# First mixer of a three-block kernel in a new order: gated-delta inverse in two halves, weight blocks by halves between scan, attention and gated levels

## What is computed

```
def token_mix(h, w_in, ...):
    p = (h @ w_in).astype(jnp.float32)
    ...
    o_a = rms_norm(fox_attention(q, k, split_heads(v, FOX_HEADS), log_f), fox_on_g)
    ...
    # gated_delta_chunked: per chunk of 64 tokens, t_mat unit lower triangular
    w = lax.linalg.triangular_solve(t_mat, kb * jnp.exp(G)[..., None], ...)
    u = lax.linalg.triangular_solve(t_mat, v * beta[..., None], ...)
    def step(state, inp):
        v_new = ui - jnp.einsum('bhcd,bhde->bhce', wi, state)
        o = einsum(qi, state) + einsum(ai_qk, v_new)
        state = state * ai[..., None, None] + einsum(ki, v_new)
    ...
    # gla_chunked (hg and gla): decayed products of q and k under a causal mask, times v
x = x + mixed @ w_out[l]
```

## Time and profile before

| | us |
|---|---|
| median of 3 runs | 1157.44 (1156.89 to 1160.16) |
| the profiled execution, its time | 1161.16 |
| its span in the trace | 1159.4 |
| PE busy, share | 95% |
| DVE busy | 70% |
| ACT busy | 52% |
| mean granted TensorE clock, of full speed | 0.956 |

### The profile page before, as it was taken

The page is one execution under the profiler, slowest core; times in us unless marked ns, Lnnn a source line. Parts: engine busy times, 40 slices in busy tenths (PEclk is TensorE's granted clock), DMA queues, the critical chain, the costliest instruction groups (busy, mean ns, idle before and its releaser), DMA issues.

```text
span 1159.4 us, 22157 instructions
## 1 busy us (share of the span) xinstructions
PE 1099.8 (95%) x9104; PEld 1069.7 (92%) x9104; DVE 809.5 (70%) x1140; ACT 598.0 (52%) x782; POOL 5.3 (0%) x15
## 2 busy tenths in 40 slices
PE   6699997799999999999999999999999899999996
PEld 5699986699999999999899999998998899999995
DVE  4557633846877777776697877778875687877775
ACT  4753341325655545544564554567666565544564
POOL 0000000000000000000000000000000000000000
PEclk9699995769999999999999999999999999999998
DMA  8333320014545455455464555543633354555531
GB/s 314 110 110 109 110 73 1 3 48 149 186 178 192 170 189 184 164 194 205 125 214 165 191 195 181 181 138 121 214 137 119 109 184 145 207 192 170 192 109 37
DMA packets 25714, 174.29 MB, mean 150 GB/s; under 512 B 3069, under 2 KB 3349, under 8 KB 5296
## 3 DMA queue, kind: packets, MB, share of 16 engines
q1 hardware_dynamic: 25088, 171.63, 42.8%
q0 software_dynamic: 560, 1.70, 0.5%
HBM read 172.26 MB, written 1.06 MB: 149 GB/s over the span
## 4 chain that ended last, share of the span: by engine, by line
PE 68%; DVE 7%; ACT 3%; issue 2%; DVEq 0%; ACTq 0%
PE PS L416 37%; PE PS L453 30%; DVE w_lo L1649 3%; ACT w_hi L1099 2%; DVE arena L2159 1%; ACT arena L1403 1%; DVE arena L2163 1%; PE PS L851 1%; DVE arena L2177 0%; DVE x L2106 0%; PE PS L856 0%; PE PS L1013 0%; DVE arena L2100 0%; DVE arena L2191 0%; DVE h_lo L1662 0%
## 5 line engine op out<-in xcount | busy, mean ns | idle before, releaser
L1649 DVE TENSOR_TENSOR w_lo<-raw,w_hi 128x2048 fp32r<-128x2048 f32 x158 | 361.3, 2288 | 103.0 <-ACT w_hi L1099 101.5
L416 PE MATMUL PS<-h_hi,w_hi 128*128 128x256 f32 x1248 | 357.3, 286 | 9.4 <-DVEq L1643 6.8
L416 PE MATMUL PS<-h_hi,w_lo 128*128 128x256 f32 x1248 | 354.8, 284 | 0.0
L416 PE MATMUL PS<-h_lo,w_hi 128*128 128x256 f32 x1248 | 354.8, 284 | 0.0
L1099 ACT ACTIVATE w_hi<-raw 128x2048 fp32r<-128x2048 f32 x158 | 300.8, 1906 | 93.4 <-PE PS L453 47.7
L416 PEld LDWEIGHTS PS<-h_hi,w_hi 128*128 128x128 f32 x1248 | 241.0, 193 | 11.2 <-DVEq L1643 7.0
L416 PEld LDWEIGHTS PS<-h_lo,w_hi 128*128 128x128 f32 x1248 | 241.0, 193 | 0.3 <-issue 0.2
L416 PEld LDWEIGHTS PS<-h_hi,w_lo 128*128 128x128 f32 x1248 | 241.1, 193 | 0.0
L453 PE MATMUL PS<-act_hi,w_hi 128*128 128x256 f32 x720 | 203.4, 284 | 2.2 <-DVE act_lo L1679 2.2
L453 PE MATMUL PS<-act_hi,w_lo 128*128 128x256 f32 x720 | 203.6, 284 | 0.0
L453 PE MATMUL PS<-act_lo,w_hi 128*128 128x256 f32 x720 | 200.9, 284 | 0.0
(11 more groups left out here) (311 smaller groups left out, 1356.0 us busy)
## 6 DMA issues: line engine op xcount, KB each, us to landing
raw<-weights SPq DMA_DIRECT2D x158, 1024.0 KB, 4.9
arena<-masks_in SPq DMA_DIRECT2D x1, 1856.0 KB, 12.7
raw<-weights SPq DMA_DIRECT2D x2, 512.0 KB, 5.8
x<-x_in SPq DMA_DIRECT2D x4, 256.0 KB, 7.2
arena<-bias_by_distance POOLq DMA_DIRECT2D x1, 1024.0 KB, 6.0
result<-x SPq DMA_DIRECT2D x4, 256.0 KB, 2.1
arena<-p_in POOLq DMA_DIRECT2D x2, 256.0 KB, 4.2
row<-row_in SPq DMA_DIRECT2D x1, 390.0 KB, 8.1
```

The lines of the kernel that those rows point to most:

```text
L416: return pe.matmul(o, lhs, rhs, start=start, stop=stop)
L1649: tt(w_lo[:, slot, :], raw[:, slot, :], w_hi[:, slot, :].bitcast(F), ALU.subtract).then_inc(lo_ready, 1)
```

## The change

It touches the first mixer alone.

- **Loads.** SP issues `w_gk` and weight block 3 ahead of `row` and the masks, and blocks 4 and 5 behind them.
- **Block order.** hg_q is block 4, fox_q, fox_k and fox_v are 5 to 7, hg_f is 8; the tables of pieces are gone, and each engine's program is a written list. PE calls `project(n, f)` for half f of block n.
- **Inverse.** Masks, copies and subtractions go by halves of four units; `gdn_cx` and `gdn_xcx` take a half g. All five levels stand between the two halves of block 8.
- **Scan, attention, levels.** Blocks 9 to 14 are multiplied here: halves of 9 to 11 and the first of 12 between the pieces of scan and attention, the second half of 12 and blocks 13 and 14 between the levels.
- **Smaller pieces.** The new state takes two DVE instructions of 128 rows in place of four of 64, and isn't made after the last chunk; the gains of fox's q and k are applied by ACT in the copy of the turned rows; norms of the heads are taken for two groups at once; ScalarE's functions are grouped so that it loads its function table 4 times behind the start in place of 7; the pairs of gla lie in banks 2 and 3 together and not in 2 to 5, which leaves 4 and 5 to the weight blocks; the first two groups are turned ahead of the last values.

```diff
-MIX_ORDER = ("small", "gdn_q", "gdn_k", "gdn_v", "hg_f", "fox_q", "fox_k", "hg_q", "fox_v", "gla_qk",
-             "gla_v", "hg_i", "gdn_z", "hg_g", "gla_g")
+MIX_ORDER = ("small", "gdn_q", "gdn_k", "gdn_v", "hg_q", "fox_q", "fox_k", "fox_v", "hg_f", "gla_qk",
+             "hg_i", "gla_v", "gdn_z", "hg_g", "gla_g")
...
+            sp.dma_start(w_gk, w_gk_in).then_inc(sem("ident_and_channel"), 16)
+            weights_in(3)
             sp.dma_start(row[:, :], row_in.partition_broadcast(P)).then_inc(sem("mix_inputs"), 16)
-            sp.dma_start(w_gk, w_gk_in).then_inc(sem("mix_inputs"), 16)
             sp.dma_start(masks, masks_in).then_inc(sem("mix_inputs"), 16)
-
+            weights_in(4)
+            weights_in(5)
...
+            def gdn_cx(lv, g):
+
+                pe.wait_ge(sem("inv_ready"), 2 * lv + g + 1)
+                pe.wait_ge(sem("ct_ready"), 2 * lv + g + 1)
+                for u in range(4 * g, 4 * g + 4):
                     last = mm(bank2(2)[:, u, :], c_t[:, u, :], inv[:, u, :])
                 last.then_inc(sem("cx"), 1)
 
-            def gdn_xcx(lv):
-                pe.wait_ge(sem("cx_copied"), lv + 1)
-                pe.wait_ge(sem("inv_t_ready"), lv + 1)
-                if lv == 0:
-                    pe.wait_ge(sem("la_keys"), 1)
-                for u in range(8):
+            def gdn_xcx(lv, g):
+                pe.wait_ge(sem("cx_copied"), 2 * lv + g + 1)
+                pe.wait_ge(sem("inv_t_ready"), 2 * lv + g + 1)
+                for u in range(4 * g, 4 * g + 4):
...
             first_columns()
             mean_of_x(0, 6, sum_1, True)
-            for n, what in enumerate(MIX_ORDER):
-                if n < 2:
-                    continue
-                for piece in before.get(n, ()):
-                    piece()
-                if n > 2:
-                    pe.wait_ge(sem(f"proj_bank_read{n % 2}"), n // 2)
-                columns(n, n % RING, 4 + n % 2, (h_hi, h_lo), what in CHANNEL_MAJOR, middle=middle.get(n, ()))
+            project(2, 0)
+            turn_small()
+            gk_product()
+            project(2, 1)
+            project(3, 0)
+            gates()
+            project(3, 1)
...
+            project(6, 1)
+            gdn_channels()
+            project(7, 0)
+            gdn_grams()
+            project(7, 1)
+            gdn_turn_decay()
+            gdn_turn_m()
+            project(8, 0)
+            for lv in range(5):
+                gdn_cx(lv, 0)
+                gdn_cx(lv, 1)
+                gdn_xcx(lv, 0)
+                gdn_xcx(lv, 1)
+            project(8, 1)
+            gdn_solve()
+            fox_turn()
+            project(9, 0)
             gdn_state_in(0)
             fox_logits(0)
             gdn_state_out(0)
+            project(9, 1)
             gdn_state_in(1)
             fox_turn_probs(0)
             gdn_state_out(1)
+            project(10, 0)
...
+            project(11, 1)
             fox_values(1)
+            project(12, 0)
             la_all()
+            la_out()
```

More of the change, by code:

```diff
@@ L178, in build @@
         e_rest = place([P, TT, HEADS])
-        e_last = place([P, TT, 2, HEADS])
+        e_last = place([P, TT, 2, 2])
         be_g = place([P, TT, HEADS])
@@ L1194, in gate_exps @@
                 act.activation(th(e_rest), PS[:, 0, 8:16], ACT.Exp)
-                act.activation(e_last.rearrange("p t c h -> p (t c h)"), PS[:, 0, 16:32], ACT.Exp) \
-                    .then_inc(once("gate_exps")[0], 1)
+                for hh in range(2):
+                    a = slice(64 * hh, 64 * hh + 64)
+                    ins = act.activation(e_last[a].rearrange("p t c r -> p (t c) r"),
+                                         PS[a, 0, 16:32].rearrange("p (u h) -> p u h", h=HEADS)[:, :, hh:hh + 3:2], ACT.Exp)
+                ins.then_inc(once("gate_exps")[0], 1)
             def gk_logs():
@@ new lines, in _ @@
+            rstd16("gdn_sums", "gdn_rstd", 1.0)
+            tokens_from(BLOCK_OF["fox_q"])
+            block_hi(7)
+            tokens_from(BLOCK_OF["fox_k"])
+            gdn_channels()
+            block_hi(8)
+            fox_squares()
+            gdn_grams()
+            tokens_from(BLOCK_OF["fox_v"])
+            gdn_turn_decay()
+            gdn_turn_m()
+            rstd16("fox_sums", "fox_rstd", 1.0 / DH)
+            block_hi(9)
+            block_hi(10)
+            for lv in range(5):
+                gdn_cx(lv, 0)
+                gdn_cx(lv, 1)
@@ L1834, in gdn_state_out @@
                 dve.wait_ge(sem("chunk_done"), c + 1)
-                for h in range(HEADS):
-                    a = slice(64 * (h % 2), 64 * (h % 2) + 64)
-                    s = state[a, h // 2, :]
-                    ins = stt(s, s, e_last[a, t, half, h:h + 1], PS[a, 2, (h // 2) * DH:(h // 2 + 1) * DH],
-                              ALU.mult, ALU.add)
+                for r in range(2):
+                    s = state[:, r, :]
+                    ins = stt(s, s, e_last[:, t, half, r:r + 1], PS[:, 2, r * DH:(r + 1) * DH], ALU.mult, ALU.add)
@@ L2006, in _ @@
[L2006 to L2026 removed]
+                    if lv in (0, 2, 4):
+                        block_lo(14 + lv // 2)
@@ new lines, in la_all, with block_lo @@
+                    if lv == 1:
+                        heads_sums(0)
+                    if lv == 3:
+                        fox_and_gdn_norm()
+                    if lv == 6:
+                        gate_gains()
+                        gdn_gate()
+            def block_lo(n):
+                split(n, n % RING)
+            gdn_scale(0, 1)
+            block_lo(3)
+            gates_in()
+            gdn_taps(0, 1)
+            gk_logits()
+            gates()
+            gate_parts()
@@ new lines, in _ @@
+            gk_logs()
+            gdn_scale(1, 2)
+            block_lo(4)
+            gdn_taps(1, 2)
+            gate_products()
+            gdn_scale(2, 3)
+            block_lo(5)
+            gdn_taps(2, 3)
+            hg_queries()
+            gdn_sums()
+            block_lo(6)
+            gdn_norms()
+            block_lo(7)
+            gdn_grams()
+            block_lo(8)
+            gdn_first_inverse()
+            gdn_a_qk()
+            fox_sums()
+            gdn_first_turned()
@@ L2027, in _ @@
+            for lv in range(5):
+                if lv < 4:
+                    gdn_next_block(lv)
+                gdn_xcx(lv)
+                if lv == 1:
+                    fox_scale()
+                if lv == 3:
+                    block_lo(9)
+            dve.memset(state, 0.0).then_inc(sem("state_ready"), 1)
             gdn_state_in(0)
```

589 lines of the change are left out of this document (331 added, 258 removed).

## The result

| | before | changed |
|---|---|---|
| median of 4 runs each, us | 1158.43 (1156.89 to 1160.16) | 1121.33 (1120.26 to 1123.97) |
| ratio, 95% interval | | 0.9683 [0.9658, 0.9708] |
| profiled execution, us | 1161.16 | 1122.38 |
| its span, us | 1159.4 | 1120.6 |
| mean granted clock | 0.956 | 0.986 |

What follows compares the result with a forecast made beforehand. PE, busy 95% of the span, bounds the kernel; time comes from its idle time and 1.2 GHz matmuls. Stretches 43.5 + 61.4 + 41.5 + 37.6 + 13.1 = 197.1 against 224.7 us give 1130 us, range 1120 to 1150.

Steps and rivals of the forecast that it cites:

- A: Stretch from block 2 to the Gram matrices: 50.1 us before, 43.5 forecast, with 11 weight halves in place of 9.
- B: Stretch from the Gram matrices to the end of fox's turns: 89.3 us before, 61.4 forecast, bounds 53 and 70.
- C: Stretch of scan and attention: 38.2 us before, 41.5 forecast with seven weight halves in it, bounds 40 and 50.
- D: Stretch of the levels: 33.0 us before, 37.6 forecast, bounded by DVE with five halves hidden, bounds 34 and 45.
- The clock decides C: Scan and attention: weight halves at every chunk hold 2.4 GHz for nearly all of the stretch, 41.5 us.
- E: Values and turns up to the first block of `w_out`: 14.05 us before, 13.1 forecast, clock unchanged at 0.50.
- 1.8 us for matmuls at 1.2 GHz: Block 2 to the Gram matrices: 1.8 us added for low-clock matmuls, within the 43.5 forecast there.
- rival 4: Taps wait for late masks, first stretch stays 52 us, and a third of scan and levels runs slow: 1153 to 1158; chance 0.05.
- terms for waits (2 + 1.3 + 2.5): PE's waits in the inverse: 2 and 1.3 us in the first level, 2.5 in the later levels.
- term 1.4 for what remains of the waits: Scan and attention: 1.4 us of waits added to 40.1 us of PE work, giving 41.5.
- Behind E: All after the first block of `w_out`: nothing of the change lies there, 914.0 us before and forecast.
- Rivals 1 and 3: Scan and levels at 1.2 GHz: a third of them, 1144 us, chance 0.22; all through, 1173 us, chance 0.08.

Runs made afterwards that it cites:

- e9: Changed kernel with five of the seven weight halves in scan and attention cut from 24 matmuls to 3: 1120.76 us, ratio 0.9681.
- e1: Kernel before, with 13 useless matmuls of zeros at each of six places of scan and attention: 1158.72 us, ratio 1.0003.
- e4: Changed kernel with the five weight halves among the levels cut from 24 matmuls to 3: 1119.54 us, ratio 0.9682.
- e2: Changed kernel where each step of the inverse waits for both halves of the one before: 1144.94 us, ratio 0.989.
- e3: Changed kernel with the old load order, row, w_gk and masks ahead of weight block 3: 1123.84 us, ratio 0.9694.
- e7b: Repeat of e7, the changed kernel with block 8's second half ahead of the inverse: 1126.4 us, ratio 0.9722.
- e7: Changed kernel with the second half of block 8 ahead of the inverse instead of behind it: 1125.54 us, ratio 0.9716.
- e8: Changed kernel with block 8's second half ahead of the inverse and 18 matmuls of zeros in levels 5 to 7: 1117.62 us, ratio 0.9657.
- e10: Changed kernel with zero matmuls in levels 5 to 7 and block 8's second half in three parts around the inverse: 1114.97 us, ratio 0.9638.

## Why the prediction was right, and where its sizes were off

The mechanism is the one put forward. Eleven halves stand in A, three in B, seven in C and five in D, and PE gets them for B's 30.6 us while C and D together grow by 6.2. The forecast missed a quarter of the gain, in the sizes listed here; nearly all of them err to the same side, so the number was not right by errors that cancel. e9 and e1 show the C part from both sides, e4 the D part, e2 the overlap in the inverse.

- **"The clock decides C"**: right. C is at 1.00 all through (before: 0.62). With five of the seven halves cut short (e9) it falls to 0.78 with no gain in time. The Trainium skill (TensorE: Matmul & The Clock Gate, Part 1: The HAM clock gate) has activity releasing the throttle; C, busy for 38.57 of 38.57 us, agrees. E does not agree with the rule taken plainly: busy all of its 11.67 us, it stands at 0.55.
- **A, term "1.8 us for matmuls at 1.2 GHz"**: mis-sized, it measured nothing; the clock was 1.00. That is 1.8 of the 2.7 us by which A was overestimated. Block 3 began 8.4 us after block 2, as the walk along DVE had it (29.1 less 20.66). The masks came in time: ACT begins to read them at 25.83, with no wait, so rival 4 fell. The forecast took A of the kernel before as 50.1; e1's profile has 47.7 for the same instructions.
- **B, terms for waits (2 + 1.3 + 2.5)**: the first two were nearly right, 2.23 and 0.80 measured, 3.0 for 3.3. The 2.5 for the later levels measured nothing, and that is nearly all of B's error. The price of the low clock, 3 us, was about right (55.67 busy for 52.4 of work). It differs between executions: e3's profile, with the same inverse, has B at 57.13. The levels took 29.8 us, 0.8 of wait included, inside the 28 to 32 given. The terms as listed add up to 61.2, not 61.4.
- **C, term 1.4 for what remains of the waits**: measured 0; and PE's own work was 38.6, not 40.1, so the sum over its prices was 1.5 too high. The margin of DVE under a half, 0.1 to 0.8 us by the working, held at every chunk.
- **D**: 38.9 for 37.6. DVE was busy 33.6 us (33.2 in the working); the 5.3 that it was not, put at 4.4, held waits of 2.2 us for the pairs and 1.9 for ACT's exponentials, a neighbour that the sum did not have, though DVE waited 2.7 for it in D of the kernel before. DVE's share of D is 0.86, as forecast.
- **E, "unchanged at 0.50"**: wrong for this execution. The last values ran partly at 2.4 GHz (the 16 records of L901 took 2.42 us; the same 16 took 3.62 before). They now follow the turns without the wait of 1.0, but that this is the reason is not shown: e3 and e7b have the same E, and in their profiles it stayed at 0.50 and took 12.71.
- **Behind E, term 0**: this is where the working was wrong in kind, since it said that nothing of the change lies there. Its window began at 262, and the 16.6 us from 245.39 stood in no stretch, though the earlier trace rows has the first 5.6 of them at 0.50. The blocks of `w_out` start at 1.00 where before they started at 0.50. Seven microseconds from the first of them hold 60 records in the changed kernel and 36 before, 24 x 0.117 = 2.8 us of the 4.0; the first row is before's, the second the changed kernel's:

```profile
245.39:252.39 7.00, 7.00 (x36) 7.00 (x37) 4.07 (x5) 3.70 (x7) 0.00 (x0) 0.57 0.00 0
```

```profile
210.64:217.64 7.00, 7.00 (x60) 7.00 (x60) 3.73 (x4) 2.45 (x4) 0.00 (x0) 1.00 0.00 0
```

How much of these 2.8 us is the change is open. e1, whose instructions from the levels on are those of the kernel before, has 48 records in the same seven microseconds; e3 and e7b, with the changed order there, have 50 and 52:

```profile
211.45:218.45 7.00, 7.00 (x50) 7.00 (x50) 3.74 (x4) 1.55 (x3) 0.00 (x0) 0.81 0.00 0
```

The other 1.2 us lie far behind, around 500 to 700 us, where before's profile has a clock of 0.99 and after's 1.00; whether the change has a part in them stays open. In sum, the errors were 2.68 + 2.69 + 2.93 - 1.30 + 1.43 + 4.05 = 12.5 us more gained than predicted, less 1.3 for the later beginning of A: 11.2 of span, and 9.7 between the medians.

Rivals 1 and 3 would have needed the low clock in C and D; it had 0 us of C and, at 0.96, about 3 of D. What stays open: what the new lists on DVE and ACT gave in A (up to 3.8 us), how much of the gain in E and behind it is the change's, and why e7's order draws one clock in one execution and the other in the next.

## What to carry to other kernels

Where a chain of small dependent steps leaves PE idle, do not look at its idle time alone. Its matmuls may run at 1.2 GHz, where each costs about double (26 weight matmuls in 5.61 us for 60 in 7.00), and independent dense work between the steps can win that back too. In the scan 12.3 us of weight products were free, where only 6.9 us had been idle. Before moving work into such a gap, measure PE's room as e1 does, with useless matmuls. That shows PE's side alone: real work also needs its operands made by other engines and a free PSUM bank. And consider splitting a dependent chain in two independent halves, so that PE works on one while the other engines work on the other: here that kept 19 us out of B.

## What was not expected of the hardware

- Work that computes nothing made two stretches faster: with 18 matmuls of zeros in the levels, D and E together took 46.27 us in place of 50.57, and E's own work 6.56 in place of 11.67.
- PE busy in every microsecond did not raise the clock by itself. Two windows, of the changed kernel's E and of its inverse:

```profile
197.00:209.00 12.00, 12.00 (x60) 11.27 (x58) 5.55 (x7) 4.07 (x5) 0.00 (x0) 0.50 0.26 89
```

```profile
84.00:90.00 6.00, 5.99 (x27) 5.70 (x28) 2.57 (x5) 2.46 (x3) 0.00 (x0) 0.50 0.00 0
```

  The first stayed at 1.2 GHz for twelve microseconds; it holds the end of the last level, the values of 64 columns and the turns. The second is the inverse's products of 128 columns.
- One order of instructions gave executions from 1118.6 to 1127.7 us. In the two that have a profile, PE has the same waits in B to a tenth of a microsecond, but behind one wait of 1.0 us the clock was at 2.4 GHz in the one and at 1.2 in the other, and B differs by 3.6 us. With the same fill in the levels, six runs that have this wait (e8) lie within 6.4 us, and five that have 0.3 in its place (e10) within 0.8. So what follows from a wait of 1 us in the profile can differ, between executions, by several times its length.
